# A transformer layer on eight cores: half of the second norm's scale and shift on ScalarE, and a third pair of banks for the first FFN units

## What is computed

```
h     = modulate(layer_norm(x), mod_x[0], mod_x[1])
mix   = token_mixer(h, ...)                       # attention and gMLP, gated, @ w_out
x_mid = post_norm(x, mod_x[2] * mix, ln1_g, ln1_b)
h2    = modulate(layer_norm(x_mid), mod_x[3], mod_x[4])
x_new = post_norm(x_mid, mod_x[5] * swiglu(h2, w_ffn_in, w_ffn_out), ln2_g, ln2_b)

modulate(y, shift, scale) = y * (1 + scale) + shift
swiglu(h, w_in, w_out): gate, up = split(h @ w_in, 2); (silu(gate) * up) @ w_out
```

## Time and profile before

| what | value |
|---|---|
| time, median of 3 runs | 980.13 us (980.02 to 981.34) |
| profiled execution, its time | 986.05 us |
| its span on the slowest core (core 2) | 984.4 us |
| spans of the 8 cores | 975.5 to 984.4 us |
| PE busy | 889.6 us (90%) |
| DVE, ACT, POOL busy | 482.3, 285.5, 239.2 us |
| costliest group: L1073, FFN up and gate matmuls | 303.8 us, 379 ns each |
| L1044, the scale and shift, 32 instructions | 13.6 us |

### The profile page before, as it was taken

One profiled execution on the slowest core, in us unless ns is written; L12 is line 12 of the kernel. 1 busy time (PEld: TensorE's weight loads), 2 busy tenths in 40 slices (PEclk: granted clock), 3 DMA queues, 4 the chain that ended last, 5 costly groups with the idle time before them and its releaser, 6 DMA issues.

```text
span 984.4 us, 15135 instructions; the slowest of 8 cores (975.5 to 984.4 us)
## 1 busy us (share of the span) xinstructions
PE 889.6 (90%) x5195; PEld 427.0 (43%) x5273; DVE 482.3 (49%) x946; ACT 285.5 (29%) x392; POOL 239.2 (24%) x282
## 2 busy tenths in 40 slices
PE   0568898889989999999998999999999999999993
PEld 0324444545544444444443444444444444444442
DVE  2147564466742366567677411122211114777774
ACT  1225545489932223332332311111111110000000
POOL 5024333266632345445443103010000000000000
PEclk9999898999999999999999999999999999999997
DMA  8999785159730023236845139962211004333231
GB/s 168 172 198 207 151 189 75 23 97 180 146 119 1 1 97 108 65 98 151 170 128 107 44 65 156 169 102 43 43 17 27 1 1 150 105 110 122 93 107 45
DMA packets 57964, 99.68 MB, mean 101 GB/s; under 512 B 20896, under 2 KB 21408, under 8 KB 57888
## 3 DMA queue, kind: packets, MB, share of 16 engines
q0 software_dynamic: 21136, 40.44, 26.4%
q1 hardware_dynamic: 36752, 58.25, 19.5%
HBM read 118.14 MB, written 16.78 MB: 137 GB/s over the span
## 4 chain that ended last, share of the span: by engine, by line
PE 71%; DMA 9%; DVE 6%; ACT 6%; issue 4%; POOL 1%; SPq 0%; another core or an unknown queue 0%; DVEq 0%; ACTq 0%; POOLq 0%
PE bank L1073 27%; PE bank L953 15%; PE bank L1204 14%; DMA arena<-wada 7%; ACT arena L812 4%; PE bank L984 4%; PE bank L488 2%; DMA arena<-xh 2%; PE bank L809 1%; PE bank L558 1%; PE bank L528 1%; DVE arena L1028 1%; PE bank L805 1%; PE bank L828 1%; DVE arena L1044 1%
## 5 line engine op out<-in xcount | busy, mean ns | idle before, releaser
L1073 PE MATMUL bank<-arena 128*128 128x512 bf16 x1380 | 303.8, 379 | 4.4 <-DVE arena L1084 1.9
L1073 PEld LDWEIGHTS bank<-arena 128*128 128x128 bf16 x1408 | 137.6, 98 | 169.7 <-issue 4.6
L953 PE MATMUL bank<-arena 128*128 128x512 bf16 x752 | 166.9, 379 | 2.2 <-DVE arena L969 0.9
L1084 DVE TENSOR_TENSOR arena<-bank,arena 128x512 bf16<-128x512 f32 x88 | 60.8, 692 | 217.6 <-PE bank L1073 209.5
L1204 PE MATMUL bank<-arena 128*128 128x512 bf16 (+1 forms) x734 | 151.5, 366 | 0.7
L1082 ACT ACTIVATE arena<-bank 128x512 f32<-128x512 f32 x88 | 52.2, 595 | 219.1 <-PE bank L1073 219.0
L953 PEld LDWEIGHTS bank<-arena 128*128 128x128 bf16 x768 | 74.9, 98 | 92.3 <-issue 2.7
L1204 PEld LDWEIGHTS bank<-arena 128*128 128x128 bf16 x748 | 73.2, 98 | 79.1
L969 DVE TENSOR_TENSOR arena<-bank,arena 128x512 f32<-128x512 f32 x64 | 43.2, 690 | 84.1 <-PE bank L953 65.5
L812 ACT ACTIVATE arena<-bank 128x1024 bf16<-128x1024 f32 x80 | 76.3, 1027 | 4.8 <-PE bank L809 4.5
L962 ACT ACTIVATE arena<-bank 128x512 f32<-128x512 f32 x64 | 36.7, 591 | 101.9 <-PE bank L953 101.9
(11 more groups left out here) (107 smaller groups left out, 869.6 us busy)
## 6 DMA issues: line engine op xcount, KB each, us to landing
arena<-xh SPq DMA_DIRECT2D x34, 512.0 KB, 6.1
arena<-wada POOLq DMA_DIRECT2D x12, 1024.0 KB, 17.2
arena<-wff POOLq DMA_DIRECT2D x11, 1024.0 KB, 10.0
xmid_d<-arena SPq DMA_DIRECT2D x16, 512.0 KB, 2.9
arena<-xmid_d SPq DMA_DIRECT2D x16, 512.0 KB, 3.8
out<-arena SPq DMA_DIRECT2D x32, 256.0 KB, 2.0
arena<-wff POOLq DMA_DIRECT2D x11, 512.0 KB, 20.0
arena<-wout SPq DMA_DIRECT2D x16, 256.0 KB, 4.5
```

The costliest lines, as they stand in the source:

```text
L953: t_mm = S.op('pe', lambda e, k=k, n=n, p=bk(bank), lhs=w[:, lo + k, :], rhs=src[:, k, tok]: e.matmul(p, lhsT=lhs, rhs=rhs, start=(k == 0) ...
L1073: rhs=h2T[:, k, tok]: e.matmul(p, lhsT=lhs, rhs=rhs, start=(k == 0), stop=(k == 7)),
L1084: fb_free[b0 + 1] = sg_free[s_] = t_act[(f, tg)] = S.op('dve', lambda e, f=f, p=bk(b0 + 1), sg=sgb[s_]: e.tensor_tensor(out=act[f][:, tok] ...
```

## The change

Two edits. In `c2_out`, the even chunks stay on DVE and the odd chunks go to ACT, as an activation with the Identity function that takes a scale and a bias for each partition. The FFN units take their banks from a list: three pairs (banks 0 and 1, 2 and 3, 6 and 7) in turn instead of two, until all steps are done, and then the four pairs as before. Banks 6 and 7 were last used in the attention part.

```diff
     def c2_out(g):
         for c in range(8):
-            t_h2[g].append(S.op('dve', lambda e, h=h2T[:, c, g * 512:(g + 1) * 512], c=c: e.tensor_scalar(
-                out=h, in0=h, scalar1=mcol(3, c, 0), scalar2=mcol(2, c, 0), op0=ALU.mult, op1=ALU.add),
-                deps=[[c2[4 * g + i]['tr'] for i in range(4)], t_modc]))
+            h = h2T[:, c, g * 512:(g + 1) * 512]
+            deps = [[c2[4 * g + i]['tr'] for i in range(4)], t_modc]
+            if c % 2 == 0:
+                t_h2[g].append(S.op('dve', lambda e, h=h, c=c: e.tensor_scalar(
+                    out=h, in0=h, scalar1=mcol(3, c, 0), scalar2=mcol(2, c, 0), op0=ALU.mult, op1=ALU.add), deps=deps))
+            else:
+                t_h2[g].append(S.op('act', lambda e, h=h, c=c: e.activation(
+                    out=h, in_=h, func=AF.Identity, scale=mcol(3, c, 0), bias=mcol(2, c, 0)), deps=deps))
...
-    gu = {'i': 0, 'pairs': 2}
+    gu = {'i': 0, 'pairs': (0, 2, 6)}
...
     def gu_pe(r, tg, fi):
         slot = r % NWR
-        b0 = (gu['i'] % gu['pairs']) * 2
+        b0 = gu['pairs'][gu['i'] % len(gu['pairs'])]
         s_ = gu['i'] % 2
         gu['i'] += 1
...
     def g2_unit():
-        b0 = (gu['i'] % gu['pairs']) * 2
+        b0 = gu['pairs'][gu['i'] % len(gu['pairs'])]
         gu['i'] += 1
...
             if not steps:
-                gu['pairs'] = 4
+                gu['pairs'] = (0, 2, 4, 6)
```

## The result

The changed kernel took 974.07 us (median of 5 runs) against 981.24 us for the kernel before in the same series (5 runs): a ratio of 0.9928, 95% interval 0.9916 to 0.994, so about 7.1 us faster. The forecast was 974.4, from a saving of 5.7. A second series run later gave 975.37 against 983.38, ratio 0.9925 (0.9909 to 0.9941).

The account below looks back on a forecast made before the run. TensorE, 90% busy, bounds the kernel and loses 7.99 us waiting on VectorE's queue. Savings of 2.50 (sharing) plus 3.44 (pairs) make 5.94 us on core 2, taken as 5.7: 980.13 to 974.4 us, range 972.7 to 977.3.

Parts of the forecast that it names:

- The chain: VectorE's queue around both norms: moving four scaling chunks off it saves 1.34 us behind group 1, 2.68 behind group 2.
- ScalarE's price: Four scaling activations cost 2.78 us on ScalarE, covered in groups 1 and 2 with 1.3 and 0.5 us to spare.
- Group 0 costs and gives nothing: Sharing the scaling behind merge unit 20 gains nothing, since it lies where TensorE doesn't wait.
- C: TensorE's wait at 493.76 us, 1.66 us, for tile 11 to leave banks 4 and 5; forecast to stay.
- A: TensorE's wait at 473.82 us, 0.72 us, for the sigmoids of unit 29; forecast to vanish.
- B: TensorE's wait at 483.47 us, 1.01 us, for VectorE's L969; forecast to shrink to 0.39.
- D: TensorE's wait at 526.00 us, 1.16 us, for tile 14 to leave banks 4 and 5; forecast to go, narrowly.
- One part alone: Each edit by itself: the third pair of banks gives 3.44 us, the sharing of the scaling 2.68 at most.
- Core 4 and the slowest core: Tile 7's transpose takes 15.3 us on core 4, so the saving there is 5.0 us; 5.7 taken overall.
- 1: Rival: the sharing gives nothing, only the pairs of banks do; 976.7 us, chance 0.16.
- 2: Rival: nothing arrives at the end, as TensorE comes earlier to FFN weights still in flight; 980 us, chance 0.07.
- 3: Rival: slower, ScalarE's queue becomes the chain ahead of the norms in groups 1 and 2; 982.7 us, chance 0.05.

Follow-up runs that it names:

- E1: Changed kernel with the sharing of the scaling alone, two pairs of banks as before: ratio 0.9952 to the kernel before, 4.7 us faster.
- E6: Changed kernel with all eight scaling chunks on ScalarE: ratio 0.9971 to the kernel before, 2.9 us faster than it, 4.5 slower than the changed kernel.
- E3: Changed kernel with group 0's scaling (behind merge unit 20) left wholly on VectorE: ratio 0.9952 to the kernel before, 4.7 us faster.
- E2: Changed kernel with three pairs of banks but all scaling on VectorE as before: ratio 0.9962 to the kernel before, 3.7 us faster.
- E5: The changed kernel run again, unedited, in the second series: ratio 0.9925 to the kernel before, 7.4 us faster.
- E8: Changed kernel, first three FFN weight loads two merge units later, output projections of tiles 12 to 15 one FFN unit later: ratio 0.9943 to the kernel before.

## Why the prediction was right, and where it was off

The time lay 0.3 us from the forecast, and that is luck: the change saved about 1.4 us more than the 5.7 worked out, and the kernel before came out at 981.24 in the median of five runs, 1.1 above the 980.13 that the saving was taken from. The two errors nearly cancel. The direction and the size of most terms were worked out rightly. By its steps:

- *What bounds it.* Right. TensorE's waits went, and the time went down by their sum: 7.4 of stretch for 7.1 of time.
- *The chain.* Right in size: 4 x 0.335 = 1.34 was worked out for a group of four, measured 3.70 - 2.41 = 1.29 in group 1, 3.65 - 2.35 = 1.30 in group 2. One wait for POOL stays in each, but "the extra lies in the first one" was read from group 2 alone. There the first L1047 takes 1.39 us and ends 0.15 after POOL's multiply. In group 1 the first takes 0.40 and the second 1.36:

```profile
454.23 1.36 DVE L1047 TENSOR_SCALAR arena<-arena 128x512 bf16<-128x512 bf16 x1
454.14 1.30 POOL L971 TENSOR_TENSOR arena<-arena 128x512 bf16<-128x512 f32 x1 [0.33 <-DVE arena L969]
```

It is POOL's add of the merge unit that holds it, and in the kernel before the second was an odd chunk (1.36 us from 467.27), one that the change moves to ScalarE. The wait went over to the next one on VectorE, so the reason that the first chunk is even was not what kept the 1.34. That one instruction waits until POOL's is done and the others take their usual time agrees with the exclusive lock that the Trainium skill describes ("SBUF — State Buffer", two separate sides).

- *ScalarE's price.* 2.78 taken, 2.93 measured; slack behind it 1.3 and 0.5 forecast, 1.43 and 0.48 measured on core 2. By the Trainium skill's figure ("ScalarE: Activation LUTs", what a table load costs) it would be 2.9, an estimate: the trace agrees. The rule of the same page of the Trainium skill (rules for kernel authors), to keep multiplies and adds on VectorE, would have cost 4.7 us here for half of them (E1, without the pairs); with all of them on ScalarE nothing is won beyond the pairs (E6).
- *Group 0 costs and gives nothing.* Wrong, and this is the step that failed. The reason given was that TensorE doesn't wait there. True, and beside the point: VectorE's chain was late behind that group and still late eight units on. In the kernel before VectorE still waits for TensorE just ahead of group 0, and then the profile names TensorE no more until the stretch:

```profile
408.60 0.69 DVE L969 TENSOR_TENSOR arena<-bank,arena 128x512 f32<-128x512 f32 x1 [1.24 <-PE bank L953]
...
410.07 3.62 DVE L1044 TENSOR_SCALAR arena<-arena 128x512 bf16<-128x512 bf16 x8
...
492.92 1.29 DVE L1007 SCALAR_TENSOR_TENSOR arena<-arena,bank 128x512 f32<-128x512 f32 x2
```

VectorE needs 13.24 us for a tile's steps where TensorE takes 13.81 for its two units (in the kernel before, VectorE's L969 at 425.65 and 438.89, TensorE's L984 at 428.21 and 442.02), so it makes up 0.57 us in each such round and can't pay back 3.6 in four. E3 puts 1.6 us on it.

- *C moves with the chain and stays.* Wrong for the same reason. On core 2 the release at C came 478.57 - 458.22 = 20.35 us behind the projection of unit 29, and 492.92 - 469.65 = 23.27 before: 2.92 earlier, of which 1.6 is group 0's and 1.3 group 1's. TensorE had only the 1.73 us of A and B to gain ahead of it, so about 1.2 of C's 1.66 went. With group 0 on VectorE (E3), C is 1.50 as predicted.
- *B leaves 0.39, D goes by 0.18.* 0.43 in E3. In the changed kernel B is 0 and D 0.05 on core 2: TensorE, no longer held at B and C, comes to D earlier too.
- *One part alone.* The pairs' 3.44 is right: E2 gave 3.7 in time, and 3.4 in loss. The sharing's 2.68 at most is wrong by group 0 again: E1 gave 4.7 in time and 4.2 in loss, which is 2.68 and 1.6.
- *Core 4 and the slowest core.* The fear was for a core whose transpose is late. It was fast enough this time (11.0 us), and where it was late, in E5 (12.2 and 12.7 us), it cost about 1 us. In E3 15.6 us cost 4.6, with the lower clock.
- *Rivals.* 1: the sharing gives nothing. Refuted by E1. 2: the gain is lost at weights in flight. No such wait shows: behind tile 15's projection every core of the changed kernel reaches the last FFN matmul in the same 286.41 us. 3: refuted at four activations. At eight the norm does wait for them, but the kernel is not slower than before.

With what the stretch of core 2 shows put in (8.0 less 0.46) the saving is 7.5 us; off the 981.24 of its own series that is 973.7, and 974.07 was measured.

## What to carry to other kernels

A short piece of work on an engine that nobody waits for now isn't free if that engine is nearly as busy as the one ahead of it: a delay is carried until the slack between them has paid it back, so look at the next place where it is waited for and at how much slack a round has. A second buffer set and a faster producer answer different waits: more banks end the waits for a bank that was used only two units ago, a shorter chain ends those for work that is late, and the two here were worth 3.4 and 4.2 us, nearly additive. When moving work to another engine, price it against the slot there, between what releases it and what stands behind it: four activations fitted into 3.4 us, eight did not, and left of 7 us of gain only the 3 or so that the pairs give by themselves. Last, a sum of idle times can miss what a long wait costs: look at the granted clock behind it.

## What the runs showed of the chip

- An in-place Identity activation with scale and bias on 128x512 bf16 in SBUF takes 2.92 to 2.93 us for four in a row and 5.74 to 5.75 for eight: 0.71 for each more. In the changed kernel VectorE works beside it, in E6 it stands idle for most of the eight.
- VectorE's four take 2.33 to 2.41 us while POOL runs an add or a multiply and 1.37 to 1.38 when it runs neither (group 3 of the changed kernel, and the row below, group 2 of E8). The extra is paid once, by the instruction that meets POOL's: the first in group 2 (1.39 us instead of 0.40), the second in groups 0 and 1 of core 2 (1.36).

```profile
514.92 1.37 DVE L1047 TENSOR_SCALAR arena<-arena 128x512 bf16<-128x512 bf16 x4
```

- A transposing DMA of one tile (SBUF to SBUF, 128x1024 bf16) lands after 2.7 to 2.9 us alone and after 7 to 18 us beside a load of 1 MB of weights from another queue. This was not expected to be so much: it is the largest spread between cores in the stretch.
- TensorE's granted clock fell from 1.00 to 0.50 in two of the waits at A: one of 3.62 us (E3, core 1) and one of 2.58 (E6, core 7). It stayed at 1.00 behind one of 3.45 (kernel before, core 4). The 48 matmuls behind the two took 13.43 and 12.19 us instead of 10.52. What decides whether it falls no run here shows.
